# A hybrid decoder layer on one core: when the cached forget rows are loaded, and how the sum of squares of x is spread

## What is computed

```python
def rmsnorm(x, g):
    xf = x.astype(jnp.float32)
    y = xf * lax.rsqrt(jnp.mean(xf * xf, axis=-1, keepdims=True) + EPS)
    return (y * g.astype(jnp.float32)).astype(x.dtype)

z = rmsnorm(x, g_attn) @ w_in            # GLA q, k, v, gates; FoX q, k, v, forget logits; two branch gates
lf_past = lf_cache[page_table]           # forget rows of the cached past, 16 pages of 128 rows x 8 heads
c_past = jnp.cumsum(lf_past, axis=1)     # enters the FoX logits of the sample tokens
merged = jax.nn.sigmoid(gate_a) * (o_gla @ w_pa) + jax.nn.sigmoid(gate_b) * (o_fox @ w_pb)
x = x + merged @ w_o
return x + (jax.nn.silu(h @ w_gate) * (h @ w_up)) @ w_down
```

## Time and profile before

| | us |
|---|---|
| median of 3 runs (lowest, highest) | 1863.02 (1861.58, 1863.72) |
| the profiled execution | 1860.16 |
| its span | 1858.5 |
| TensorE busy in it | 1830.5 (98%) |
| VectorE busy | 967.3 (52%) |
| ScalarE busy | 687.8 (37%) |
| GpSimd busy | 23.2 (1%) |

### The profile page before, as it was taken

How to read it: one execution, slowest core, us unless ns; L and a number is a source line. 1 busy time by engine, 2 the same in 40 slices (tenths; PEclk the granted TensorE clock), 3 DMA queues, 4 the chain that set the end, 5 groups by cost and what they waited for, 6 DMA issues and landing times.

```text
span 1858.5 us, 31129 instructions
## 1 busy us (share of the span) xinstructions
PE 1830.5 (98%) x12950; PEld 1798.1 (97%) x12950; DVE 967.3 (52%) x1360; ACT 687.8 (37%) x948; POOL 23.2 (1%) x56
## 2 busy tenths in 40 slices
PE   8999999999999999999999999999999999999996
PEld 7899999999999999999999999999999999999996
DVE  6765465456446544665554444444444444444454
ACT  5443333333333343344433333333333333333353
POOL 3000000000000000000000000000000000000000
PEclk9999999999999999999999999999999999999998
DMA  6464556437555644454454445444454445544443
GB/s 207 161 216 151 171 173 197 158 128 222 161 169 174 203 135 150 165 187 143 131 170 147 135 147 172 148 147 135 148 172 148 147 135 147 172 148 148 135 141 110
DMA packets 129343, 295.26 MB, mean 159 GB/s; under 512 B 15770, under 2 KB 59298, under 8 KB 129202
## 3 DMA queue, kind: packets, MB, share of 16 engines
q1 hardware_dynamic: 121666, 284.54, 48.6%
q10 hardware_dynamic: 7504, 8.72, 1.3%
q0 software_dynamic: 32, 0.01, 0.0%
HBM read 283.25 MB, written 9.97 MB: 158 GB/s over the span
## 4 chain that ended last, share of the span: by engine, by line
PE 98%; DVE 0%; DMA 0%; ACT 0%; issue 0%; DVEq 0%; SPq 0%
PE banks L1072 31%; PE banks L1074 31%; PE banks L1073 31%; PE banks L1085 3%; PE banks L1082 1%; DMA weights_raw<-in_w_project 0%; PE banks L1310 0%; PE banks L1312 0%; PE banks L1311 0%; PE banks L1180 0%; DVE gates L1059 0%; PE banks L1105 0%; DVEq L111 0%; ACT L634 0%; ACT L633 0%
## 5 line engine op out<-in xcount | busy, mean ns | idle before, releaser
L653 DVE TENSOR_TENSOR weights_low<-weights_raw,weights_high 128x1024 fp32r<-128x1024 f32 (+2 forms) x530 | 607.6, 1147 | 569.2 <-ACT weights_high L445 565.9
L445 ACT ACTIVATE weights_high<-weights_raw 128x1024 fp32r<-128x1024 f32 (+2 forms) x530 | 524.9, 991 | 624.3 <-PE banks L1074 610.3
L1072 PE MATMUL banks<-a_high,weights_high 128*128 128x320 f32 x2224 | 705.0, 317 | 0.0
L1074 PE MATMUL banks<-a_high,weights_low 128*128 128x320 f32 x2224 | 687.2, 309 | 0.0
L1073 PE MATMUL banks<-a_low,weights_high 128*128 128x320 f32 x2224 | 687.0, 309 | 0.0
L1072 PE MATMUL banks<-b_high,weights_high 128*128 128x320 f32 x1664 | 514.9, 309 | 0.1
L1074 PE MATMUL banks<-b_high,weights_low 128*128 128x320 f32 x1664 | 514.2, 309 | 0.0
L1073 PE MATMUL banks<-b_low,weights_high 128*128 128x320 f32 x1664 | 514.1, 309 | 0.0
L1072 PEld LDWEIGHTS banks<-a_high,weights_high 128*128 128x128 f32 x2224 | 417.6, 188 | 11.9 <-issue 8.3
L1073 PEld LDWEIGHTS banks<-a_low,weights_high 128*128 128x128 f32 x2224 | 418.1, 188 | 0.3
L1074 PEld LDWEIGHTS banks<-a_high,weights_low 128*128 128x128 f32 x2224 | 417.4, 188 | 0.0
(11 more groups left out here) (214 smaller groups left out, 675.5 us busy)
## 6 DMA issues: line engine op xcount, KB each, us to landing
weights_raw<-in_w_gate_up SPq DMA_DIRECT2D x176, 512.0 KB, 3.4
weights_raw<-in_w_project SPq DMA_DIRECT2D x160, 512.0 KB, 3.4
weights_raw<-in_w_down_a SPq DMA_DIRECT2D x64, 384.0 KB, 3.1
weights_raw<-in_w_down_b SPq DMA_DIRECT2D x64, 320.0 KB, 2.9
weights_raw<-in_w_merge SPq DMA_DIRECT2D x32, 512.0 KB, 3.3
weights_raw<-in_w_out SPq DMA_DIRECT2D x32, 512.0 KB, 3.5
area<-in_cache_kT SPq DMA_DIRECT2D x128, 64.0 KB, 2.6
area<-in_cache_v SPq DMA_DIRECT2D x128, 64.0 KB, 2.7
```

The costliest lines, as they stand in the source:

```text
L445: act.activation(high[:, u % SLOTS, 0:n], raw[:, u % SLOTS, 0:n], ACT.Copy).then_inc(on["high_ready"], 1)
L653: dve.tensor_tensor(low[:, u % SLOTS, 0:n], raw[:, u % SLOTS, 0:n], high[:, u % SLOTS, 0:n].bitcast(F32), ALU.subtract).then_inc(on["low_r ...
L1072: pe.matmul(bank(b, 0, T), w_high, x_high[:, k, :], start=first and n == 0, stop=False, skip_group_check=True)
L1074: done = pe.matmul(bank(b, 0, T), w_low, x_high[:, k, :], start=False, stop=last and n == tiles - 1, skip_group_check=True)
```

## The change

The 16 loads of forget rows stand behind the weight loads of s = 12 to 15 instead of s = 6 to 9, and the wait before the first of them is for all eight squares in place of `x_sum_spread`. VectorE, behind the split of the unit s = 4 (u = 6), waits for GpSimd's sum, adds it to its own and adds the two halves of 320 columns (new L703 and L704). TensorE multiplies ones with that one 128x320 tile in one product instead of four.

```diff
--- before.py
+++ after.py
@@ -283,11 +283,11 @@
                     u = U_PROJECT + TURN_UNITS * i + s
                     if u > SLOTS:
                         load(u, w_project[u - U_PROJECT])
-                    if i == 0 and s == 6:
-                        sp.wait_ge(on["x_sum_spread"], 1)
+                    if i == 0 and s == 12:
+                        sp.wait_ge(on["x_squared"], KT // 2)
                         sp.wait_ge(on["x_low_ready"], KT)
-                    if i == 0 and 6 <= s < 10:
-                        for n in range(4 * (s - 6), 4 * (s - 6) + 4):
+                    if i == 0 and 12 <= s < 16:
+                        for n in range(4 * (s - 12), 4 * (s - 12) + 4):
                             sp.dma_start(lf_past[:, n % PAGES, FH * (n // PAGES):FH * (n // PAGES) + FH], cache_lf[page[n], :, :].rearrange("o k h -> (o k) h")
                                          ).then_inc(on["lf_past_landed"], 16)
                     if s == 5:
@@ -697,8 +697,12 @@
                     for c in ((3,), (5, 7))[s]:
                         dve.wait_ge(on["x_squared"], c + 1)
                         link(dve.tensor_tensor(squares_x[:, 1, :], squares_x[:, 1, :], squares_x[:, c, :], ALU.add))
-                    if s == 1:
-                        dve.sem_inc(on["x_summed"], 1)
+                if s == 2:
+
+                    dve.wait_ge(on["x_summed_pool"], 1)
+                    link(dve.tensor_tensor(squares_x[:, 1, :], squares_x[:, 1, :], squares_x[:, 0, :], ALU.add))
+                    dve.tensor_tensor(gates[:, 16, :], squares_x[:, 1, 0:T], squares_x[:, 1, T:2 * T], ALU.add
+                                      ).then_inc(on["x_summed"], 1)
                 if s == 4:
                     dve.wait_ge(on["x_sum_spread"], 1)
                     link(dve.tensor_scalar(mean_x, bank(7, 0, T), 1.0 / D, EPS, ALU.mult, ALU.add))
@@ -1088,11 +1092,7 @@
                 if s == 4 and n == 0:
                     pe.wait_ge(on["ones_ready"], 1)
                     pe.wait_ge(on["x_summed"], 1)
-                    pe.wait_ge(on["x_summed_pool"], 1)
-                    for c in range(2):
-                        for t in range(2):
-                            last = add(bank(7, 0, T), ones[:, :], squares_x[:, c, t * T:(t + 1) * T], start=c + t == 0, stop=c + t == 2)
-                    last.then_inc(on["x_sum_spread"], 1)
+                    add(bank(7, 0, T), ones[:, :], gates[:, 16, :], start=True, stop=True).then_inc(on["x_sum_spread"], 1)
                 if (s, n) in ((5, 4), (22, 4), (23, 4), (24, 4)):
                     h = (5, 22, 23, 24).index(s)
                     if h == 0:
```

## The result

| | before | after |
|---|---|---|
| median, first comparison (6 runs each) | 1863.33 (1861.07 to 1863.72) | 1854.03 (1853.08 to 1855.41) |
| median, second comparison (24 and 5 runs) | 1861.63 (1860.19 to 1864.10) | 1854.41 (1854.04 to 1855.08) |
| profiled execution, its span | 1860.16, 1858.5 | 1853.83, 1852.1 |

The ratio of the first comparison is 0.9954 (95% interval 0.9941 to 0.9967), that of the second 0.9962 (0.9948 to 0.9976). The prediction was wrong in size.

What follows compares the result with a forecast made beforehand. TensorE, busy 1830.5 of 1858.5 us, was taken as the bound. The product's -1.62 and the wait for K's -3.56 gave -5.18 us, so 1863.02 became 1857.8 us, range 1855.8 to 1861.7.

Steps and rivals of the forecast that it cites:

- The product: TensorE near 34 us: one product of ones in place of four, 2.45 us becoming 0.83, so -1.62 us.
- The adds: Two new adds on VectorE behind the split of u = 6: 1.4 us together, upper bound 3.6.
- a margin of 0.8 us where I had 1.2: At the product of ones: sum ready at 32.8, TensorE there at 33.98, margin 1.2 us, no wait.
- the case in which VectorE is second: New adds beside GpSimd's L403: each add could wait 0.79 us, so 0.5 us of the gain would go.
- The queue on SyncE: Load of u = 9, issued at 38.91 behind x_sum_spread, would wait only for its slot, free before 27 us.
- The wait for K goes: TensorE behind tile 1 of s = 9: K read in time, so the whole 3.56 us go.
- rival B: The 3.4 us at s = 9 are TensorE's own instruction-stream pause and stay: 1861.4 us; chance 0.13.
- the 0.6 that I had: At s = 9: K ready at 52.73, TensorE there at 53.47; margin 0.6 us with 0.10 for the signal.
- From the profiled execution to the median: The median's 2.86 us above the profiled execution was carried to the changed kernel: 1863.02 - 5.18 = 1857.8.
- A: Slow adds: TensorE waits 1.1 us for the sum, 0.5 for K; gain 3.6, time 1859.4; chance 0.13.
- C: TensorE gives back 1.1 us at a later first-turn wait, s = 12 to 20: 1858.9; chance 0.07.
- D: Pages hold up weight loads of u = 15 to 18; TensorE waits 24.8 us: 1882.6; chance 0.04.

Runs made afterwards that it cites:

- e3: Kernel before with only the pages moved to s = 12 to 15 behind the wait for the squares, four products kept: 1855.99 us against 1861.88, ratio 0.9971.
- e5: The changed kernel once more, no edit, beside the kernel before: 1854.41 us (5 runs) against 1861.63, ratio 0.9962.
- e2: Kernel before with only the sums on VectorE and one product, pages left at s = 6 to 9: 1859.52 us against 1861.88, ratio 0.9985.
- e7: Changed kernel with 12 needless VectorE operations ahead of the read of K, so TensorE waits 3.2 us: 1860.09 us (11 runs).
- e4: Kernel before with pages left at s = 6 to 9 but behind the wait for the squares, four products: 1855.78 us, ratio 0.9969.
- e1: The kernel before once more, no edit, for a second trace: 1861.48 us (11 runs), ratio 0.9998.
- e9: A further trace of the unchanged kernel before; no run time given, 195.85 us from product of ones to second turn.
- e10: Another trace of the unchanged kernel before: execution of 1859.64 us, 194.58 us from product of ones to second turn.
- e11: Another trace of the unchanged kernel before; no run time given, 195.79 us from product of ones to second turn.
- e8: Changed kernel with 23 needless VectorE operations ahead of the read of K, so TensorE waits 7.3 us: 1864.01 us (11 runs).
- e6: Changed kernel with 7 needless VectorE operations ahead of the read of K, so TensorE waits 1.4 us: 1856.56 us (8 runs).

## Why the prediction was wrong in size

- **The product, -1.62 us.** Right: 0.83 us of TensorE in the trace. The cleanest price is between e3 and e5, both without a wait: 189.57 - 187.96 = 1.61 us in distance, 1855.99 - 1854.41 = 1.58 between medians. Alone (e2) it was -2.4 (-4.5 to -0.9) us.
- **The adds, 1.4 us on VectorE.** Right: 30.55 to 31.98 is 1.43 us, and no wait of TensorE, which came at 32.80, a margin of 0.8 us where I had 1.2. GpSimd's first select was the one to suffer. GpSimd's timeline before, and then after:

```profile
30.08 0.29 POOL L395 TENSOR_SCALAR_AFFINE_SELECT gates<-ones 128x128 f32<-128x128 f32 x1
```

```profile
29.40 1.38 POOL L395 TENSOR_SCALAR_AFFINE_SELECT gates<-ones 128x128 f32<-128x128 f32 x1
...
31.96 2.85 POOL L403 TENSOR_SCALAR_AFFINE_SELECT gates<-gates 64x64 f32<-64x64 f32 x3
```

The split of u = 6 on VectorE, after:

```profile
29.40 1.23 DVE L653 TENSOR_TENSOR weights_low<-weights_raw,weights_high 128x1024 fp32r<-128x1024 f32 x1
```

The same select and the same split in e7:

```profile
30.17 0.29 POOL L395 TENSOR_SCALAR_AFFINE_SELECT gates<-ones 128x128 f32<-128x128 f32 x1
```

```profile
30.17 1.36 DVE L653 TENSOR_TENSOR weights_low<-weights_raw,weights_high 128x1024 fp32r<-128x1024 f32 x1
```

The select L395 took 1.38 us where it had taken 0.29, nearly all of it beside the split of u = 6, and the three L403 2.85 where the earlier trace rows has 2.36; the select L398 between them went the other way, from 0.86 to 0.46. In e7, whose code is the same here, the select took 0.29 and the split 1.36 in place of 1.23. This agrees with the rule of the Trainium skill ("SBUF — State Buffer", section "Who interferes with whom") that whichever of the two comes second is blocked. I had weighed only the case in which VectorE is second. No wait of TensorE came of it.
- **The queue on SyncE.** Right, and shown by e4: the wait alone held up the load of u = 9.
- **The wait for K goes, -3.56 us.** The mechanism was right, rival B (a pause of TensorE's own, called "issue") is refuted by the changed trace, and the margin, 52.30 less 51.49 = 0.8 us, is near the 0.6 that I had (0.56 in e5). **The size is the term that failed.** I read the price of the wait in one execution, the one in which the granted clock had stayed at 1.00 behind it. In the four other traces of the kernel before it went to 0.50, at a price of 1.5 to 2.4 us each time; over the five the wait cost 3.56 + 1.7 = 5.3 us. I had put this part at nothing without a reason. With -1.62 this makes -6.9, and e5 measured -7.2.
- **From the profiled execution to the median.** In part the same error. I added the 2.86 us by which the median lay above the profiled execution to the forecast for the changed kernel, as though any kernel had them. The profiled execution of the changed one is 1853.83 and its median 1854.03. The sum by the trace alone, 1854.98, would have been in the runs' range, though it carries the late start of that execution (33.98 against 32.80), which isn't the kernel's. The 2.86 us were a sign, which I did not read, that most executions lost time which the trace did not show. Over the 49 later runs the median lies only 1.6 us above the profiled execution; I put the other 1.3 down to having had three runs, which isn't shown.
- **Rivals A, C and D.** None came: no wait at the product of ones, none between 60 us and the tail, and u = 15 to 18 in time.
- **Open.** The first comparison says 9.3 us, its interval 6.1 to 11.0, the second 7.2. The six runs of before in the first have a median 1.6 us above that of the 49 runs taken in the two later comparisons (1861.77). The start, up to the product of ones, varies too, from 31.39 to 34.12 us in the five traces of before; the traces don't say how much of the 9.3 is that. How often the clock falls in unprofiled executions isn't counted. The mean granted clock of these runs is on record, to three digits: 0.997 in all 11 runs of the changed kernel, and in the 49 runs of before 0.997 twice, 0.996 31 times and 0.995 16 times. This agrees with a fall in most of them; but 0.996 alone doesn't prove one, since e3, without a fall in its trace, has it in three of seven runs. Why the clock stayed at 1.00 in the first trace, behind the same wait, is open.

## What to carry to other kernels

A wait of TensorE of some 3 us wasn't priced by its length alone here: 5.3 us for 3.4. Look at the granted clock in narrow stretches behind it, in more than one execution, and where the runs' median lies well above the profiled execution, look for what that execution was spared before you carry the difference over to the forecast. A wait on SyncE held up every load that stood behind it in program order, the load of u = 9 until 38.91 where it went out at 26.41 and 28.68 without: place such a wait as late as its data allow, or wait for the earliest signal that makes the transfer safe, which here was one line.

## What was not expected of the hardware

- After 3.1 to 3.7 us without work the granted clock of TensorE was 0.50 for a while in six of seven traces (e1, e2, e7, e9, e10, e11, and not in the first of before), after 7.3 us it was too, and after 1.4 us it was 1.00 (one trace each). It fell while TensorE still waited in e2, e8, e9, e10 and e11, at the restart in e7, and some 1 us behind the restart in e1. The same program with the same wait can come out either way.
- The time at half clock was 3.4 us (e1, e7, e10), 6.8 us (e2, e9, e11) or 10.2 us (e8), added up from stretches of 1 us. In the traces of before the loss was 1.5 to 2.4 us; what lay inside the wait cost nothing.
- GpSimd's reads of SBUF beside VectorE's split of two inputs: 1.38 us in place of 0.29 us for one select of 128x128 (1.37 in e2, e5, e6 and e8), and once the other way round, the split 1.36 us and the select 0.29 (e7).
